# A linear attention's norm and gating behind a barrier, decay products regrouped, and a barrier joined late

## The reference, cut to what matters

```
o_b = (ob_f + flip_t(ob_b))                                   # GLA, 4 heads of 128
o_b = rms_norm(o_b, gla_gain).reshape(B, T, WIDTH_BV) * silu(gb)
decay = exp(-exp(-softplus(-(w0[d] + tanh(wlr) @ w2[d])) - 0.5))   # RWKV, d = 0, 1
a = sigmoid(a0[d] + alr @ a2[d])
kd = kc * (1 + (a - 1) * k_a)
y_f, y_b = the two scans over (r, decay, kd, vc, -kk, kk * a)
merged = gates[0] * (o_a @ w_po_a) + gates[1] * (o_b @ w_po_b) + gates[2] * (o_c @ w_po_c)
x = x + gt1 * (merged @ w_out)
```

## Time and profile before

| what | value |
|---|---|
| median of 3 runs | 1979.22 us (1973.89 to 1980.21) |
| profiled execution | 1970.69 us, span 1968.9 us |
| mean granted TensorE clock | 0.965 |
| busy: PE, DVE, ACT, POOL | 90%, 49%, 38%, 14% of the span |
| chain that ended last | PE 73%, DVE 12%, ACT 6%, issue 5%, POOL 3% |
| phase 3, layer 0 | 396.0 to 622.3 us |
| phase 3, layer 1 | 1359.4 to 1583.6 us |

### The profile page before, as it was taken

How to read it: one execution, slowest core, us unless ns; L and a number is a source line. 1 busy time by engine, 2 the same in 40 slices (tenths; PEclk the granted TensorE clock), 3 DMA queues, 4 the chain that set the end, 5 groups by cost and what they waited for, 6 DMA issues and landing times.

```text
span 1968.9 us, 42031 instructions
## 1 busy us (share of the span) xinstructions
PE 1777.5 (90%) x18403; PEld 1490.8 (76%) x18403; DVE 958.1 (49%) x1699; ACT 748.1 (38%) x1325; POOL 275.1 (14%) x457
## 2 busy tenths in 40 slices
PE   4899888688898999999989989987888989999998
PEld 2899555456665989999989975554666679899998
DVE  1526436575555554343342444465765447443333
ACT  3334436424334343332243443534332443533321
POOL 2000003165330000000000000042744000000000
PEclk9999999889899999999999999998999989999999
DMA  8443233202403537653433432321041245344342
GB/s 280 148 128 118 73 112 105 85 7 67 131 3 120 191 108 192 171 151 103 132 124 110 139 93 87 126 89 49 3 154 44 67 137 157 86 128 128 102 132 77
DMA packets 268525, 219.51 MB, mean 111 GB/s; under 512 B 7289, under 2 KB 259608, under 8 KB 267704
## 3 DMA queue, kind: packets, MB, share of 16 engines
q1 hardware_dynamic: 264816, 203.67, 34.2%
q0 software_dynamic: 3312, 13.09, 1.9%
q10 hardware_dynamic: 216, 0.06, 0.0%
HBM read 210.77 MB, written 6.03 MB: 110 GB/s over the span
## 4 chain that ended last, share of the span: by engine, by line
PE 73%; DVE 12%; ACT 6%; issue 5%; POOL 3%; DMA 1%; ACTq 0%; SPq 0%; DVEq 0%; POOLq 0%
PE bank L590 13%; PE bank L595 13%; PE bank L591 12%; PE bank L649 8%; PE bank L1255 3%; PE bank L1257 3%; PE bank L1256 3%; PE bank L655 3%; PE bank L1032 2%; PE bank L549 2%; PE bank L646 1%; PE bank L776 1%; PE bank L813 1%; PE bank L574 1%; DVE scr_rounded L1984 1%
## 5 line engine op out<-in xcount | busy, mean ns | idle before, releaser
L591 PE MATMUL bank<-scr_rounded 128*128 128x384 f32 x1344 | 452.3, 337 | 0.0
L591 PEld LDWEIGHTS bank<-scr_rounded 128*128 128x128 f32 x1344 | 253.8, 189 | 1.3
L590 PE MATMUL bank<-scr_rounded 128*128 128x384 f32 (+1 forms) x672 | 227.1, 338 | 13.9 <-ACT scr_rounded L1507 13.3
L590 PE MATMUL bank<-scr_rounded,gate_rounded 128*128 128x384 f32 (+1 forms) x672 | 227.5, 339 | 11.2 <-ACT scr_rounded L1507 9.3
L649 PE MATMUL bank<-h,ring 128*128 128x384 f32 x576 | 212.4, 512 | 15.9 <-DVEq L368 9.0
L595 PE MATMUL bank<-scr_rounded 128*128 128x384 f32 (+1 forms) x672 | 222.1, 337 | 0.0
L595 PE MATMUL bank<-scr_rounded,gate_rounded 128*128 128x384 f32 (+1 forms) x672 | 222.1, 336 | 0.0
L1984 DVE TENSOR_TENSOR scr_rounded<-ring,gate_rounded 128x2048 fp32r<-128x2048 f32 (+3 forms) x65 | 135.4, 2083 | 154.1 <-ACT gate_rounded L1496 153.4
L1984 DVE TENSOR_TENSOR scr_rounded<-ring,scr_rounded 128x2048 fp32r<-128x2048 f32 (+1 forms) x65 | 135.3, 2082 | 136.8 <-ACT scr_rounded L1496 135.1
L649 PEld LDWEIGHTS bank<-h,ring 128*128 128x128 f32 x576 | 106.8, 195 | 93.5 <-issue 36.0
L1496 ACT ACTIVATE gate_rounded<-ring 128x2048 fp32r<-128x2048 f32 (+3 forms) x65 | 113.6, 1747 | 152.5 <-PE bank L595 64.5
(11 more groups left out here) (410 smaller groups left out, 3133.2 us busy)
## 6 DMA issues: line engine op xcount, KB each, us to landing
ring<-in_w_in_dram SPq DMA_DIRECT2D x56, 1024.0 KB, 5.4
ring<-in_w_ada_dram SPq DMA_DIRECT2D x48, 1024.0 KB, 5.4
ring<-in_w_ffn_in_dram SPq DMA_DIRECT2D x88, 512.0 KB, 5.2
ring<-in_w_ffn_out_dram SPq DMA_DIRECT2D x32, 704.0 KB, 4.5
ring<-in_w_out_dram SPq DMA_DIRECT2D x8, 1024.0 KB, 5.1
ring<-in_w_po_a_dram SPq DMA_DIRECT2D x4, 1024.0 KB, 6.1
ring<-in_w_po_b_dram SPq DMA_DIRECT2D x4, 1024.0 KB, 6.4
ring<-in_w_po_c_dram SPq DMA_DIRECT2D x4, 1024.0 KB, 9.3
```

Source lines behind the costliest of these rows:

```text
L590: pe.matmul(o, w_hi[:, k, :], right[0][k], start=k == 0, stop=False)
L591: pe.matmul(o, w_lo[:, k, :], right[0][k], start=False, stop=False)
```

## The change

It has these parts.

1. GLA's norm and gating move from before barrier 2 to behind it, on PE behind `grams(0)`, on ACT ahead of `decays(2)`, on DVE behind `begin(0)`. A new semaphore, `gla_gated`, holds PE's first projection of these heads, and ACT's `factor(0, 0)`, which overwrites the gates.
2. `loras(3)` moves ahead of the state's turn (`s0T`), and with `FILLS[0]` now 0 it stands next to `loras(2)`. `FILLS` goes from 8, 8, 0, 0 to 0, 10, 2, 1 at its first places, and three later zeros, the places before `turned_values(1)`, `(2)` and `(3)`, become 1. The sum stays 47.
3. On POOL the last product of `factors(2)` and `factors(3)` moves behind `substitution(1)` as `read_factors`.
4. On DVE the copy of `s0T` moves ahead of `inverses(0)`.
5. `barrier` is split into `arrive` and `join`. PE arrives at barrier 3, runs gate(2,0) and gate(2,1), and joins after them.

```diff
+        def arrive(eng, who):
             eng.drain().then_inc(phase[who], 1)
+        def join(eng, who, l, k):
             for other in phase:
                 if other != who:
                     eng.wait_ge(phase[other], l * NPHASE + k + 1)
-        FILLS = (8, 8, 0, 0, 1, 1, 1, 1, 1, 1, 2, 1, 1, 0, 1, 1, 1, 1, 1, 1, 2, 1, 1, 0, 1, 1, 1, 1, 1, 1, 0, 1, 1, 0, 1, 1, 1, 0, 0, 0, 0)
+        FILLS = (0, 10, 2, 1, 1, 1, 1, 1, 1, 1, 2, 1, 1, 1, 1, 1, 1, 1, 1, 1, 2, 1, 1, 1, 1, 1, 1, 1, 1, 1, 0, 1, 1, 1, 1, 1, 1, 0, 0, 0, 0)
@@ side_steps
+                        if work[2] == 1 and j == 0:
+                            pe.wait_ge(S["gla_gated"], told("gla_gated", l, 4))
@@ tensor
                 loras(0)
-                for hh in range(4):
-                    pe.wait_ge(S["gla_osq"], told("gla_osq", l, hh + 1))
-                    ...
                 loras(1)
...
                 grams(0)
+                for hh in range(4):
+                    pe.wait_ge(S["gla_osq"], told("gla_osq", l, hh + 1))
+                    pe.wait_ge(*room())
+                    b = item("A", "obms", l, hh)
+                    pe.matmul(b[:, 0:T], ones, ob_square[:, hh, :], start=True, stop=True).then_inc(psum_ready, 1)
                 loras(2)
                 fill(next(steps))
+                loras(3)
                 pe.wait_ge(rwkv_in, 16 * (l + 1))
                 ...
-                loras(3)
                 fill(next(steps))
...
-                barrier(pe, "pe", l, 3)
+                arrive(pe, "pe")
                 side[0] = side_steps(side_plan(l, 4))
                 finish(l, 4)
+                join(pe, "pe", l, 3)
@@ gpsimd, factors(g)
-                    gp.tensor_tensor(at[:, :, 1, :], at[:, :, 1, :], c6(pc[:, hp, :]), mult).then_inc(*tells("rw_factors"))
+                    if g not in (2, 3):
+                        read_factors(g)
+                def read_factors(g):
+                    hp, d = groups[g]
+                    at = ar[hp % 2][d]
+                    gp.wait_ge(S["rw_terms"], told("rw_terms", l, g + 1))
+                    gp.tensor_tensor(at[:, :, 1, :], ...).then_inc(*tells("rw_factors"))
...
                 substitution(1)
+                read_factors(2)
+                read_factors(3)
                 bonus_rows(0)
@@ scalar
                 rates(0)
+                decays(1)
+                exps(0)
+                rates(1)
+                exps(1)
+                side_work("phase", l, 2)
+                barrier(act, "act", l, 2)
                 for hh in range(4):      # Ln, then Exp, of the four heads, as before
...
-                decays(1)
-                exps(0)
-                rates(1)
-                exps(1)
-                side_work("phase", l, 2)
-                barrier(act, "act", l, 2)
...
                 merged_blocks(0)
+                act.wait_ge(S["gla_gated"], told("gla_gated", l, 4))
                 factor(0, 0)
@@ vector
                 keys(0)
-                for hh in range(4):      # the gating, moved as it is
-                    ...
                 dve.wait_ge(x_out, 16 * (l + 1))
...
                 grams(0)
                 begin(0)
+                for hh in range(4):
+                    side_work("obms", l, hh)
+                    dve.wait_ge(S["gla_rstd"], told("gla_rstd", l, hh + 1))
+                    o = pb[:, 4 + hh, :]
+                    stt(out=o, in0=o, scalar=P(l, "gla_gain"), in1=ob_scale[:, hh, :], op0=mult, op1=mult).then_inc(*step())
+                    dve.wait_ge(*last())
+                    tt(o, o, pb[:, 8 + hh, :], mult).then_inc(*tells("gla_gated"))
                 logs(2)
...
                 terms(3)
-                inverses(0)
                 side_work("s0T", l)
                 ...
                 cp(h0.rearrange("p a b -> p (a b)"), b[:, 0:512]).then_inc(*empties("s0T", l))
+                inverses(0)
                 grams(1)
```

More of the change, by code:

```diff
@@ L292, in step_kernel @@
             "gla_abs", "gla_log", "gla_beta", "gla_exps", "gla_scaled", "gla_x", "gla_xe", "gla_z", "gla_far", "gla_near_v", "gla_near_a",
-            "gla_osq", "gla_rstd",
+            "gla_osq", "gla_rstd", "gla_gated",
             "rw_lora", "rw_kksq", "rw_kkr", "rw_logs", "rw_exps", "rw_terms", "rw_empty", "rw_cc", "rw_off", "rw_w", "rw_inv",
@@ L359, in step_kernel @@
                    gla_z=14, gla_far=FAR - 1, gla_near_v=1, gla_near_a=1, gla_osq=4, gla_rstd=4, rw_lora=1, rw_kksq=4, rw_kkr=4,
-                   rw_logs=8, rw_exps=8, rw_terms=8, rw_empty=1, rw_cc=4, rw_off=4, rw_w=4, rw_inv=4, rw_zt=4, rw_zc=4, rw_zn=4, rw_h=8, rw_q=8, rw_keys=8, rw_kd=8, rw_factors=8, rw_bonus=4,
+                   gla_gated=4, rw_logs=8, rw_exps=8, rw_terms=8, rw_empty=1, rw_cc=4, rw_off=4, rw_w=4, rw_inv=4, rw_zt=4, rw_zc=4, rw_zn=4, rw_h=8, rw_q=8, rw_keys=8, rw_kd=8, rw_factors=8, rw_bonus=4,
                    rw_ysq=4, rw_yr=4, shifted=15, branch_merged=16)
@@ L364, in step_kernel @@
         NPHASE = 5
-        def barrier(eng, who, l, k):
+        def arrive(eng, who):
             eng.drain().then_inc(phase[who], 1)
+        def join(eng, who, l, k):
             for other in phase:
@@ L371, in barrier @@
                     eng.wait_ge(phase[other], l * NPHASE + k + 1)
-        FILLS = (8, 8, 0, 0, 1, 1, 1, 1, 1, 1, 2, 1, 1, 0, 1, 1, 1, 1, 1, 1, 2, 1, 1, 0, 1, 1, 1, 1, 1, 1, 0, 1, 1, 0, 1, 1, 1, 0, 0, 0, 0)
+        def barrier(eng, who, l, k):
+            arrive(eng, who)
+            join(eng, who, l, k)
+        FILLS = (0, 10, 2, 1, 1, 1, 1, 1, 1, 1, 2, 1, 1, 1, 1, 1, 1, 1, 1, 1, 2, 1, 1, 1, 1, 1, 1, 1, 1, 1, 0, 1, 1, 1, 1, 1, 1, 0, 0, 0, 0)
         def side_plan(l, k):
@@ L902, in _ @@
                 loras(0)
-                for hh in range(4):
-                    pe.wait_ge(S["gla_osq"], told("gla_osq", l, hh + 1))
-                    pe.wait_ge(*room())
-                    b = item("A", "obms", l, hh)
-                    pe.matmul(b[:, 0:T], ones, ob_square[:, hh, :], start=True, stop=True).then_inc(psum_ready, 1)
                 loras(1)
@@ L1399, in factors @@
                     c6 = lambda ap: ap.rearrange("p (c q) -> p c q", c=6)
-                    at, bt = ar[i][d], BT[i][d]
+                    bt = BT[i][d]
                     gp.wait_ge(S["rw_kd"], told("rw_kd", l, g + 1))
@@ L1407, in factors @@
                         gp.tensor_tensor(kdp[i][0], kdp[i][0], kdp[i][1], add).then_inc(*step())
-                    gp.tensor_tensor(at[:, :, 1, :], at[:, :, 1, :], c6(pc[:, hp, :]), mult).then_inc(*tells("rw_factors"))
+                    if g not in (2, 3):
[4 more added lines that the diff above has]
+                    gp.wait_ge(S["rw_terms"], told("rw_terms", l, g + 1))
+                    gp.tensor_tensor(at[:, :, 1, :], at[:, :, 1, :], pc[:, hp, :].rearrange("p (c q) -> p c q", c=6), mult).then_inc(*tells("rw_factors"))
                 def bonus_rows(hp):
@@ L2426, in _ @@
                 keys(0)
-                for hh in range(4):
-                    side_work("obms", l, hh)
-                    dve.wait_ge(S["gla_rstd"], told("gla_rstd", l, hh + 1))
-                    o = pb[:, 4 + hh, :]
-                    stt(out=o, in0=o, scalar=P(l, "gla_gain"), in1=ob_scale[:, hh, :], op0=mult, op1=mult).then_inc(*step())
-                    dve.wait_ge(*last())
-                    tt(o, o, pb[:, 8 + hh, :], mult).then_inc(*step())
                 dve.wait_ge(x_out, 16 * (l + 1))
```

## The result

The changed kernel takes 1957.42 us (median of five, 1955.2 to 1964.39), against 1974.22 (1973.56 to 1980.21) for the kernel before in the runs beside it: ratio 0.9908, 95% interval 0.9882 to 0.9933. That is 16.8 us faster; the forecast was 5.9. The forecast time, 1973.3, is 15.9 us above the measured one; 5.0 of these come from its starting point, a median of 1979.22 from three runs where the comparison has 1974.22. The profiled execution has 1955.46 us and a span of 1953.6, 15.3 less than before's.

The account below looks back on a forecast made before the run. The prediction took TensorE (PE) as the bound, with gains only from its gaps and low clock. Per layer +2.4 - 1.7 + 0.9 - 4.7 = -3.1; over two layers, adjusted, -5.9 from 1979.2 gives 1973.3 us, range 1956 to 1986.

Parts of the forecast that it names:

- the stall: Ahead of the first block squares: PE waits some 8 us until DVE empties the bank of po(1,0).
- the late join: At barrier 3: two gates run inside PE's 4.50 us wait; -4.7 us per layer, bounds 3.0 and 6.0.
- account A: Main account: the stall occurs as forecast; total 1966 to 1981 us, chance 0.58.
- B: Rival: first projection emptied in time, no stall; first squares at Gram +35.5, total 1948 us, chance 0.12.
- the rest of the stage: From the second block squares on: three deferred steps cost +0.9 us, a vanished low-clock stretch gives -1.7, per layer.
- Norm and gating out of the stage: Before barrier 2: the barrier falls 6.8 us earlier, at 389.2; PE still waits some 4.6 us there.
- The same work behind the barrier: After the first Gram: DVE gates from +9.9 to about +14.5 us; PE waits 3.3 us for it.
- The ten fills in one piece: Before the first block squares: po(1,0) emptied at Gram +34.0, 3.7 us lost at low clock, squares at +48.0.
- What is won back by the second squares: Second block squares come 25.5 us after the first, not 30.5; 2.4 us late in absolute time.
- The contention: DVE's gating shares SBUF interfaces with POOL, lengthening POOL's substitution by about 2 us, with 8 us of room.
- C: Rival: po(1,0) released at +38.5 and the stage can't absorb it; net +4.5 us a layer, 1988, chance 0.20.
- D: Rival: the late join gives nothing because following work waits for split weights; +9.4 us, about 1983, chance 0.10.

Follow-up runs that it names:

- e3: Changed kernel, with VectorE releasing the first projection's bank, po(1,0), right after logs(3) instead of behind inverses(0): 1945.25 us.
- e6: Kernel before, with only the norm and gating moved behind barrier 2 and the first Gram products: 1973.22 us against 1978.82, ratio 0.9975.
- e7: Changed kernel, with the read factors of the third and fourth group back in their old places on GpSimd: 1956.71 us, ratio 0.9903.
- e1: Kernel before, with four fill steps moved from behind transitions(n) to ahead of turned_values(n): 1977.55 us against 1974.39, ratio 1.0016.
- e4: Kernel before, with only the late join (both gates between arrival at barrier 3 and the wait): 1965.77 us, ratio 0.9958.
- e9: Changed kernel, with four fill steps put back ahead of the first block squares, as in the old split: 1973.01 us against 1976.51, ratio 0.9976.
- e5: Kernel before, with only the new split: four fill steps moved from ahead of the first block squares to four empty places: 1962.64 us against 1978.82, ratio 0.9931.
- e8: e3 with gate product gate(1,2) put ahead of the first projection: 1944.36 us.
- e10: Changed kernel, with barrier 3 back ahead of the last two gate products instead of the late join: 1966.68 us, ratio 0.9953.
- e11: e3 with one conditioning product drawn ahead of the first projection, its bank emptied at once by ScalarE: 1940.92 us against 1976.51, ratio 0.9824.
- e2: Changed kernel, with the four fill steps ahead of turned_values(n) put back behind transitions(n): 1961.96 us, ratio 0.9942.

## Why the prediction was right in kind and too small

The sign, the stall and the late join came as forecast; the size did not, 16.8 us where the forecast had 5.9. The measured 1957.42 lies outside account A's own range, 1966 to 1981, and inside the wide one, 1956 to 1986, by 1.4 us. That low end was there for a part of B, in which the stall is missing, and the stall is there. So it is luck that the range holds the result. The step that failed is the rest of the stage, told below.

**Norm and gating out of the stage: right.** The piece from the head's output to the Gram is 6.7 and 8.2 us shorter; forecast 6.8. Without the +5.2 us ahead of it, the Gram stands at 389.3; forecast 389.2. PE still waits 5.95 us; forecast some 4.6. It comes out at the low level, as forecast (the first 48 matmuls take 1.56 us).

**The same work behind the barrier: right, with a wait twice as long.** VectorE's timeline after:

```profile
402.92 0.76 DVE L2463 SCALAR_TENSOR_TENSOR arena<-arena,par,gate 128x384 f32<-128x384 f32 x1 [3.68 <-ACT gate L1850]
...
412.56 0.96 DVE L2289 TENSOR_TENSOR_SCAN x<-cst,arena 128x384 f32<-128x384 f32 x1 [0.55 <-ACT arena L1731]
...
414.64 0.63 DVE L2307 SCALAR_TENSOR_TENSOR scr<-scr 128x384 f32<-128x384 f32 x1
...
417.00 1.35 DVE L2307 SCALAR_TENSOR_TENSOR scr<-scr 128x384 f32<-128x384 f32 x1
...
419.80 0.68 DVE L2477 COPY scr<-bank 128x512 f32<-128x512 f32 x1
...
424.33 0.56 DVE L1998 SCALAR_TENSOR_TENSOR gtmp<-gtmp,bank 128x384 f32<-128x384 f32 x1
```

Gating starts at Gram + 8.4 (forecast 9.9) and ends at + 13.8 (14.5). PE waits 6.50 and not 3.3 since it came there at + 7.5 and not at + 11.2: the obms matmuls were done at + 5.5 (forecast 7.3), and the loras and the state's turn took 2.0 us where I had 3.9. I had kept TensorE at the low level there, and it was granted 0.74 in the mean from 394.52 to 402.00.

**The ten fills in one piece: the mechanism is shown, its term was 5 us too large.** The stall is there with the named releaser, 6.79 and 6.78 us (forecast some 8). e3 takes away only what makes it wait, and it goes; e6 has the first po ahead of `loras(3)`, and it has none. The release came at Gram + 30.4 (424.33 + 0.56), not + 34.0. `logs(3)` starts at + 18.0 (forecast 19.2), and from there to the s0T copy DVE needs 7.2 us where the forecast had 10.1, its own timeline of before carried over. Neither has idle time in that piece; the operations themselves were slower. VectorE's timeline before, the same two operations:

```profile
417.03 1.35 DVE L2285 SCALAR_TENSOR_TENSOR scr<-scr 128x384 f32<-128x384 f32 x1
...
422.27 1.34 DVE L2285 SCALAR_TENSOR_TENSOR scr<-scr 128x384 f32<-128x384 f32 x1
```

They took 0.63 and 1.35 after. The slow ones of both kernels begin only when GpSimd is at its 128x384 factors, from 416.58 and from 416.62 (its timeline is below). After, VectorE's chain starts 0.9 us sooner behind the Gram and the factors 1.6 us later, so more of it runs ahead of them. I had moved that chain as a block, with a neighbour's slowing in it that belonged to the old order. No run isolates this cause. Behind the stall, the two steps at the low level took 4.84 us for 2.74, 2.1 lost where I had 3.7. So S1 stands at + 43.0 and not + 48.0.

**What is won back by the second squares: too large, since another engine took over the bound.** S1 to S2 is 27.6 and 28.5 (forecast 25.5, before 30.5). GpSimd's timeline after has both terms of the forecast, and VectorE's behind it shows why they did not pass:

```profile
439.84 0.83 POOL L1401 TENSOR_TENSOR scr<-scr,cst 128x384 f32<-128x384 f32 x1 [13.58 <-DVE scr L2391]
...
459.41 2.28 POOL L1427 TENSOR_TENSOR scr<-scr,arena 128x384 f32<-128x384 f32 x2
```

```profile
456.06 1.02 DVE L2361 TENSOR_TENSOR x<-bank,cst 128x384 f32<-128x384 f32 x2 [5.50 <-PE bank L1037]
...
461.80 1.12 DVE L2339 STREAM_TRANSPOSE scr<-cst 128x512 f32<-128x512 f32 x1
```

GpSimd goes on 2.3 us behind S1, before 5.6 (forecast 3.2 sooner), and its substitution is done 21.9 us behind S1, at 459.41; before it took 27.0 (456.89). That is the 5.1 us of the forecast. But VectorE had waited 5.50 us for a product of PE and comes to `inverses(1)` only at 461.80, from its own list and not from GpSimd; before it waited 1.27 us for GpSimd at 457.03. So "just fits" was wrong, and with the read factors back (e7) the squares come no later. Head to S2 is 0.4 and 0.6 us shorter than before, where I had 2.4 longer. So up to here the headline move, with the stall that it brings, comes out at nothing: its barrier gain is real, and the waits for the gating and for the bank take it. e3 is where it is paid out.

**The rest of the stage: the step that failed most.** The prediction put it at +0.9 for three deferred steps and -1.7 for the low clock, -0.8 in all. Measured, S2 to the last head variance is -7.0 and -2.5. Over all kernels, the five with the old number of steps in each block (before, e1, e4, e6, e9) need 99.7 us in the mean from S2 to S4 (ten layers, 97.3 to 103.9), the six with the full new one (after, e3, e5, e7, e8, e10) 94.0 (twelve layers, 91.7 to 96.1); the two sets don't meet. e11, whose list of side work differs, has 93.7 and 92.2, and of e2's layers one lies in each set (98.3, 94.2). Against it stand +0.9 from S4 to the last variance (58.0 to 58.9). That is -4.8 per layer. Two things were missing. First, I priced one wait of 1.04 us at each place and so one step as worth 1.04. The two waits for ScalarE in this stretch are gone as forecast (2.0 us in layer 0), but PE's idle time falls by 5.2 in the mean (13.8 to 16.9 before, 8.9 to 10.7 then): in layer 0 the "issue" time falls too, from 3.8 to 1.4 us, and the wait for ScalarE's `modrow` from 3.6 to 2.9. Second, I took a short wait's price as its length. The granted clock of the stretch is 0.90 to 0.96 with the old split and 0.95 to 1.00 with the new. The table lets the two be weighed. Layer 1 of before and of after have the same 0.96; idle time falls by 6.0 there, and PE's busy time grows from 82.0 to 85.1, about the two steps more (2 x 1.33), so all of the 2.9 us won is idle time. In layer 0, with 0.91 and 1.00, idle time falls by 3.6 and busy time by 4.2 in spite of these two steps, so the clock gives some 6.9. In the mean of the two sets idle time gives 5.2 us and the clock an estimated 3.1 (busy time falls by 0.5 with 2.7 of work more). So the waits weigh more.

**The late join: near.** Forecast -4.7 per layer, bounds 3.0 to 6.0; measured -3.5 and -4.4, and -5.8 and -5.6 alone. Over all rows the last column is 16.5 us in the mean without the join (five kernels) and 11.6 with it (eight), some 4.8 us less.

**The contention: as far as the trace went.** GpSimd's timeline after, two operations of one shape, then the end of the substitution:

```profile
402.04 0.33 POOL L1387 TENSOR_TENSOR cst<-cst,lora 128x72 f32<-128x72 f32 x1
...
413.70 0.60 POOL L1387 TENSOR_TENSOR cst<-cst,lora 128x72 f32<-128x72 f32 x1
...
416.62 1.32 POOL L1413 TENSOR_TENSOR x<-x,arena 128x384 f32<-128x384 f32 x1
```

The substitution ends at Gram + 22.1, before at + 20.5: 1.6 us later, where the prediction estimated 2. At 402.04 VectorE is idle (it waits 3.68 us until 402.92), and at 413.70 it is at an operation with two SBUF inputs. The trace agrees with the Trainium skill's rule ("GPSIMD Engine Reference", 1. Specifications), by which the two engines share SBUF interfaces and contend when VectorE has two SBUF inputs; the page has no figure for it. VectorE pays too: the gating pair takes 0.76 and 0.63, before 0.62 for the first. As foreseen, nobody waited for it.

**The sum.** Per layer, forecast +2.4 - 0.8 - 4.7 = -3.1; measured -0.4 - 7.0 - 3.5, with rounding -11.0, and -0.6 - 2.5 - 4.4, with rounding -7.6. The parts do not add up: alone they give 0.25 points (e6), 0.69 (e5) and 0.42 (e4), 1.36 together, and the whole gives 0.92. What is missing, 0.44, is about what e3 wins back by removing the stall (0.51): an estimate, since each of these ratios is uncertain by 0.14 to 0.27 points. Of the rivals, B's price (no stall, 1948) is about what e3 reaches, but B did not occur in the changed kernel, nor did C's release (+ 37) or D's wait for split weights.

## What to carry to other kernels

Interleaved filler work has a price that depends on where it stands: put it where the bound engine waits, also for waits of a microsecond, and count idle time and busy time of the whole stretch, since one covered wait can come back as another (e1) and the clock moves with them. When a block of work moves behind a barrier, follow the first thing that needs it, and then who empties that thing's buffer and at which call: a release that sits at a fixed place in another engine's order can cost all that the move won. When a chain of one engine is carried over to a new order, look for what slowed or released it in the old one: here the same VectorE chain took 10.1 and 7.2 us, and the engine that bounds the second squares changed.

## What the runs showed of the hardware

**The clock of untouched code.** The stretch from the start to the first GLA output is the same in all kernels, and takes 368.8 us in the profile of before and 371.1 to 376.2 in the twelve others, with some 22 us at the low level in the first and 22 to 38 in the others (2 x (1 - granted clock) x length). So a comparison of two single profiles carries some 5 us, here 5.2, that the change has not made; before's profiled execution, 1970.69, also lies below the medians of 1974 to 1979.

**A table load that waited.** ScalarE's timeline after, behind the barrier:

```profile
397.76 1.28 ACT L1847 ACT_TABLE_LOAD   x1 [5.03 <-PE bank L1145]
...
401.07 1.28 ACT L1850 ACT_TABLE_LOAD   x1
```

I had put the first table load under the obms matmuls. It began only when the first of their results was there, with the operation that needs it, after 5.03 us of idle time. In this trace Ln and Exp of one group cost a load of 1.28 us each, and the next operation starts within 0.02 us of the load's end (399.05 and 402.36).
